# A small scratch tensor 32 columns wider: every tensor allocated behind it moves 128 bytes up in SBUF

## The reference

```
x = first_block(x, p, ...)       # RMS norm, a wide projection, four mixers side by side
                                 # (conformer convolution, forgetting attention, short convolution,
                                 # multiscale pooling), output projection, then a 1024-4096-1024 MLP with
                                 # squared ReLU, then a gated embedding
return second_block(x, ...)      # RMS norm, a wide projection, sliding-window attention with sinks beside
                                 # gated linear attention in chunks, gated merge, output projection,
                                 # then a gated feed-forward of 2816 with a causal convolution of width 3
```

## Time and profile before

| | us |
|---|---|
| median of 3 runs | 1540.04 |
| the profiled execution's own time | 1541.17 |
| its span, first to last instruction | 1539.4 |
| PE busy | 1475.8 (96%) |
| DVE busy | 836.5 (54%) |
| ACT busy | 571.0 (37%) |
| POOL busy | 263.1 (17%) |

### The profile page before, as it was taken

One profiled execution on the slowest core, in us unless ns is written; L12 is line 12 of the kernel. 1 busy time (PEld: TensorE's weight loads), 2 busy tenths in 40 slices (PEclk: granted clock), 3 DMA queues, 4 the chain that ended last, 5 costly groups with the idle time before them and its releaser, 6 DMA issues.

```text
span 1539.4 us, 17873 instructions
## 1 busy us (share of the span) xinstructions
PE 1475.8 (96%) x7048; PEld 1204.6 (78%) x7048; DVE 836.5 (54%) x1150; ACT 571.0 (37%) x836; POOL 263.1 (17%) x169
## 2 busy tenths in 40 slices
PE   7988999999999999889999989999999999999998
PEld 6756676888888887766778868888887888888887
DVE  5598756443333345675548762734444565544564
ACT  4334444442323224432355465422224343322310
POOL 4243334320201001432014401300002000000000
PEclk9998999999999999998899999999999999999999
DMA  6221122233233332221121011233332133333231
GB/s 220 70 68 42 55 69 70 81 122 97 88 103 96 96 96 83 69 69 55 56 69 56 28 55 42 82 97 96 97 98 95 64 115 96 110 96 96 92 100 69
DMA packets 35987, 129.18 MB, mean 84 GB/s; under 512 B 4008, under 2 KB 4136, under 8 KB 35904
## 3 DMA queue, kind: packets, MB, share of 16 engines
q1 hardware_dynamic: 35904, 128.04, 26.2%
HBM read 125.91 MB, written 2.10 MB: 83 GB/s over the span
## 4 chain that ended last, share of the span: by engine, by line
PE 86%; DVE 8%; ACT 3%; issue 2%; POOL 2%; DMA 0%; SPq 0%; DVEq 0%; POOLq 0%; ACTq 0%
PE P L1011 25%; PE P L1012 24%; PE P L1013 24%; DVE ACC L1780 2%; PE P L1243 2%; PE P L1032 1%; PE P L1033 1%; PE P L1034 1%; PE P L1090 1%; POOL AC L2254 1%; PE P L1129 1%; POOL DD L2254 0%; PE P L1226 0%; PE P L1286 0%; ACT WH L1323 0%
## 5 line engine op out<-in xcount | busy, mean ns | idle before, releaser
L1011 PE MATMUL P<-AH,WH 128*128 128x512 f32 x1104 | 447.9, 406 | 24.8 <-DVE AL L1634 11.5
L1013 PE MATMUL P<-AH,WL 128*128 128x512 f32 x1104 | 435.4, 394 | 0.0
L1012 PE MATMUL P<-AL,WH 128*128 128x512 f32 x1104 | 435.4, 394 | 0.0
L1323 ACT ACTIVATE WH<-WR 128x1024 fp32r<-128x1024 f32 x233 | 245.0, 1052 | 341.3 <-PE P L1013 330.4
L1629 DVE TENSOR_TENSOR WL<-WR,WH 128x1024 fp32r<-128x1024 f32 x216 | 273.0, 1264 | 170.4 <-ACT WH L1323 170.1
L1011 PEld LDWEIGHTS P<-AH,WH 128*128 128x128 f32 x1104 | 210.9, 191 | 77.1 <-issue 26.5
L1013 PEld LDWEIGHTS P<-AH,WL 128*128 128x128 f32 x1104 | 210.5, 191 | 45.4
L1012 PEld LDWEIGHTS P<-AL,WH 128*128 128x128 f32 x1104 | 211.0, 191 | 42.4 <-issue 1.0
L1011 PE MATMUL P<-FH,WH 128*128 128x512 f32 x432 | 168.0, 389 | 0.0
L1012 PE MATMUL P<-FL,WH 128*128 128x512 f32 x432 | 168.0, 389 | 0.0
L1013 PE MATMUL P<-FH,WL 128*128 128x512 f32 x432 | 168.0, 389 | 0.0
(11 more groups left out here) (300 smaller groups left out, 1891.9 us busy)
## 6 DMA issues: line engine op xcount, KB each, us to landing
WR<-in_ws SPq DMA_DIRECT2D x233, 512.0 KB, 3.6
out<-Y SPq DMA_DIRECT2D x8, 256.0 KB, 2.0
H<-in_xT SPq DMA_DIRECT2D x3, 512.0 KB, 8.2
C<-in_const SPq DMA_DIRECT2D x1, 946.5 KB, 11.0
H<-in_xT SPq DMA_DIRECT2D x2, 256.0 KB, 4.4
PR<-in_pT SPq DMA_DIRECT2D x1, 512.0 KB, 5.0
PM<-in_params SPq DMA_DIRECT2D x1, 121.5 KB, 2.8
GKU<-in_gku SPq DMA_DIRECT2D x1, 32.0 KB, 10.4
```

Source lines behind the costliest of these rows:

```text
L1011: e.matmul(P, wh, xh, start=start, stop=False)
L1012: e.matmul(P, wh, xl, start=False, stop=False)
L1013: ins = e.matmul(P, wl, xh, start=False, stop=stop)
L1323: e.activation(m.WH[:, c % NW, :], m.WR[:, c % NRAW, :], ACT.Copy).then_inc(*at.up("w_hi", "w_hi", c))
```

## The change

NR grows from 416 to 448 columns, the limit of what `roots` may hand out rises from 392 to 424, and the sinks and the decays move behind the new limit, 32 columns (128 bytes) further up in NR. By the widening `base` goes up by 128 bytes, and with it all tensors placed by `at`; those placed by `fixed` stay. The instructions of each engine, their order, their shapes and their waits are the same before and after.

```diff
-        self.NR = f("NR", [128, 416])
+        self.NR = f("NR", [128, 448])
...
-            assert self.nrcol <= 392
+            assert self.nrcol <= 424
...
-        e.activation(m.NR[:, 400:416], halves(flat(m.BC), 128)[:, :, 127], ACT.Exp, scale=1.0 / 16).then_inc(
+        e.activation(m.NR[:, 432:448], halves(flat(m.BC), 128)[:, :, 127], ACT.Exp, scale=1.0 / 16).then_inc(
...
-        e.tensor_scalar(m.NR[:, 392:400], m.p("sinks", 0, 8), -1.0, None, ALU.mult).then_inc(
+        e.tensor_scalar(m.NR[:, 424:432], m.p("sinks", 0, 8), -1.0, None, ALU.mult).then_inc(
...
-        sink = m.NR[:, 392 + 2 * j:394 + 2 * j]
+        sink = m.NR[:, 424 + 2 * j:426 + 2 * j]
...
-                e.scalar_tensor_tensor(m.ST2[:, n, s], m.ST2[:, n - 1, s], m.NR[:, 400 + 4 * hh + n:401 + 4 * hh + n], ps,
+                e.scalar_tensor_tensor(m.ST2[:, n, s], m.ST2[:, n - 1, s], m.NR[:, 432 + 4 * hh + n:433 + 4 * hh + n], ps,
```

## The result

The changed kernel takes 1553.9 us in the median of four runs (1551.22 to 1556.13); the kernel before takes 1540.61 (four runs, 1539.27 to 1541.32). The ratio is 1.0088, with a 95% interval of 1.0069 to 1.0107: slower by 13.3 us, where no change was forecast. The profiled execution of the changed kernel took 1554.61 us, its span is 1552.8.

The account below looks back on a forecast made before the run. The prediction took PE's matmul pace to bound the kernel. All terms were 0 us, so the changed kernel's median was forecast at 1540.0 us, range 1535.5 to 1545, with 0.79 on no measurable change.

Parts of the forecast that it names:

- What bounds the kernel: Whole kernel: PE busy 1475.8 of 1539.4 us and 86% of the last chain, so nearly all time is matmuls' pace.
- Nothing issued or reordered, NR's columns: Same instructions and waits, sinks and decays moved 128 bytes within NR: both terms 0 us.
- TensorE: 2016 matmuls whose moving operand shifts by 128 bytes while weights WH and WL stay: taken as 0 us.
- the nearest row (GKU against C): Matmuls at L1165 (weights GKU) against L1061 (both operands C): 587 against 590 ns, read as no effect of address.
- The count: Matmuls at L1011, L1012 and L1013 with a moved operand: 3 x 672 = 2016.
- The bounds of that step: At most 13.3 ns (32 columns) for each of 2016 moved matmuls: 26.9 us either way.
- the faster end: Rival: moved matmuls win back 13.3 ns each, 26.9 us, giving 1513 us, or 1533 for a quarter; chance 0.06.
- DVE, ACT: VectorE and ScalarE work on moved tensors: 0 us each, with 3.3 us for DVE kept as an end either side.
- POOL: POOL's work 0 us; slower rival: sums of squares at L2254 grow 16%, 4.9 us, giving 1545 us; chance 0.06.
- Transfers: Last output DMA from Y, which moves: 0 us, bound 0.13 us either side, page's rule estimating 0.1 us gain.
- The clock: Stretches at 1.2 GHz: median moves 1 us either way; with DVE's 3.3 us, chance 0.04 faster, 0.05 slower.
- What would show it: Timeline checks: FH and AH matmuls stay 226.7 ns apart, L1780 744 ns, L2254 1262 ns; differing paces prove the first rival.

## Why the prediction was wrong, point by point

**What bounds the kernel** was right. PE is 87% of the chain after, and the time came through its pace and not through a wait.

**Nothing issued or reordered, NR's columns:** 0, right. The 128 free bytes alone give a ratio of 1.0094, the change 1.0088.

**TensorE, the step that failed.** The prediction said "I take 0, since it is what the nearest row (GKU against C) says". The term is 12.8 us. Two things went wrong. The first is the format of that row: it is a matmul in plain fp32 of 430 ns, and the runs in plain fp32 take 429.2 ns at distances of 0, 128 and 32 alike, so the row could not show the effect. That the same L1165 went from a distance of 128 to 0 with the change and kept its floor of 587 ns says the same, and its quick steps are 429 ns from start to start in both traces. That the row compared durations of single instructions was not what failed: the section on the profile before holds that the duration doesn't tell the cost, but FH's mean duration rose from 389 to 395 ns, nearly all of the 6.35 ns that the step rose by. The second is the reading of the earlier trace rows. The prediction saw that "Both operands sit 128 bytes above a multiple of 256", and took it for a statement on the operand alone. It did not set WH's 128 beside it, though the layout had all three in one table; the two rows had the same distance to the weights, 0, and said nothing of any other.

**The count** of 2016 moved matmuls leaves out the 18 with CHh, CLl, DH and DL, 0.1 us.

**The bounds of that step** held: 26.9 us either way, of which 12.8 came true. The worst distance measured costs 13.4 ns (240.0 at 20 bytes against 226.6), about the bound's 13.3, by luck: the bound was made from 32 columns, and no run bears that out as the mechanism. But only the faster end became a rival. A slower kernel through the matmuls' pace had no chance of its own, although the term said "either way", and the range ended at 1545. With an unknown of 26.9 us on both sides that rests on one row of another format, the slower side had to have the same chance as the faster one at least.

**DVE, ACT:** 0, right; L1780 keeps 744, L2172 752, L1336 616. **POOL:** 0, right, and the rival fell with it: L2254 has 1259 at best where 1388 was the point from which it would have decided. **Transfers:** out<-Y lands in 2.0 us as in the earlier trace rows. The rule of the Trainium skill (page "DMA: Bandwidth & Descriptors", section "How a descriptor splits into AXI transactions") would give 0.1 us by the prediction's estimate, which is under what this row resolves; no run here shows it.

**The clock:** put at 1 us either way on a median, and it gave some 1 us to the slower side. That bound is not safe: with `base` 64 bytes up, spans at a mean of 0.980 are 5.2 us longer than at 0.983. **What would show it** was right as a test: "a pace of FH that differs from AH's" was named as the proof of a pace that depends on the start, and the trace shows just that, 233.5 against 226.7, on the other side of zero.

No layout tried beats the kernel before: distance 0 is the best found for rows of 512 columns, and the three kernels that keep it at other addresses (all tensors moved, NR of 352 columns, C and PM first) equal it.

## What to carry to other kernels

When tensors are moved or padded, and the kernel lives on long rows of `fp32r` matmuls 512 columns wide with a weight load each, write down the distance between each moving operand and its weights modulo 256 bytes, and keep it at 0; here a scratch 128 bytes wider cost 0.9%, and putting two tensors elsewhere took it back whole. Read the pace per operand from start to start, before and after any change of layout; here the mean duration of each operand's group moved with it. A row of another number format is no neighbour for such a question, however near its address.

## What the runs showed that was not expected

- The pace of the 512-wide `fp32r` matmul hangs on the distance between the two operands modulo 256 bytes: 226.7 ns at 0, 228.9 at 64, 232.8 to 234.5 at the other multiples of 32, 240.0 at 20. The Trainium skill, page "TensorE: Matmul & The Clock Gate", section "Step-by-step: what each phase is for", says that the weight load and the stream read SBUF by two ports of their own and that a load takes no bandwidth from the running matmul. The measurement shows that the pace hangs on the two addresses together all the same, by up to 13.4 ns per matmul, and it decides; by what mechanism, no run here shows.
- It does not show in plain fp32 (429.2 ns at 0, 128 and 32), nor as a loss with 256 or fewer moving columns, and between 512 and 384 columns its sign depends on the width (with 480 columns a distance of 128 is the faster one, 213.3 against 216.5 ns; with 496 the slower, 226.7 against 223.4).
- Among matmuls at distance 0, one weight block in three or four at 128 slows two steps (232.6 to 234.0 ns), one moving operand in four slows one (234.3). With other patterns this does not hold, and a row at distance 0 can take ten matmuls to settle.
